# One decoder step on one core: the second feed-forward layer of the last 520 tokens in seven products instead of eight, with low parts of the weights kept from the first half

## The chip, the cores and the metric

One core of a Trainium2 chip runs the whole program. The metric is device time in microseconds (us) of one execution. Three executions of the kernel before took 1424.0, 1428.06 and 1427.56 us; the median is 1427.56 us.

## What is computed

A one-layer decoder on 1024 prompt tokens and 8 sample tokens: an input projection, a gated linear attention and a differential attention beside it (the sample tokens read a paged cache), an output projection, and a feed-forward block. The change touches the last part alone:

```python
    x = x + jnp.einsum('bte,ed->btd', mix, p['w_out'])
    h2 = rmsnorm(x, p['norm_ffn_g'])
    u = jnp.square(jax.nn.relu(jnp.einsum('btd,df->btf', h2, p['w_up'])))
    x = x + jnp.einsum('btf,fd->btd', u, p['w_down'])
```

D_MODEL is 1024, D_FF 4096; all data are fp32.

## The kernel before

**Three products for one.** Each fp32 operand is split into a high part (a copy into fp32r by ScalarE) and a low part (what is left, a subtraction by VectorE). A tile product is then three matmuls, high times high, high times low, low times high (`split_matmuls`, L85 to L87).

**Two blocks of tokens.** Block A is tokens 0 to 511, block B the last 512 prompt tokens and the 8 sample tokens. Inside the program's order comes first the front (input projection, about 430 us), then `feed_forward(part=0)` for A, with attention, recurrence, the keys and the values of the cache done beside it by `beside(tick)` calls, and last `feed_forward(part=1)` for B, with nothing beside it. In B a tile of tokens is two halves p of 256 and 264 columns.

**One block of the feed-forward.** First the output projection, 8 tiles `out`. Then eight groups g: four tiles `up` (x = 0 to 3; 8 k-tiles each, weights `w_up`), and eight tiles `down` (o = 0 to 7; the group's four k-tiles, weights `w_down`), which VectorE adds to the running sum `xt` (L2254). A group of B is 192 matmuls up and 192 down.

**Who makes what, in each group.** SyncE loads the `w_up` tiles into `raw_up` (L1871), ScalarE's queue the `w_down` tiles into `raw_dn` (L2102). For each tile ScalarE makes the high part (`split_high` L2080, `down_high` L2095) and VectorE the low part (`split_low` L2084, `down_low` L2190). After an `up` tile VectorE applies relu and the norm's factor (L2236), ScalarE squares (L2153) and makes the high part `uh` (L2155), VectorE the low part `ul` (L2243). Both blocks split all weights anew.

**What sets the order.** Every engine runs its list in the order in which it is written, and waits on counting semaphores. PSUM has 8 banks; B uses four of them in turn, and a bank is free once VectorE has read it (`take`, `freed`). In B the norm's factors are made behind the first `up` tile: L1975, L2195, L2184 (GpSimd), L2200, L1982, and last the copy `rb2` (L2145), which the first relu waits for.

**Beside A in the last third of its time** run the cached values: 32 units of four 256 KB pages (`vr`, L2555), each unit two groups of four matmuls (L2634); the ring holds two units' pages.

**The end.** `turn_y` transposes `xt` (L2045), ScalarE copies to `y` (L2113; two buffers, so the third copy waits for the first store), SyncE stores (L1896, L1898).

## Time and profile before

| | |
|---|---|
| three executions, us | 1424.0, 1428.06, 1427.56 |
| median, us | 1427.56 |
| profiled execution, span, us | 1424.1 |
| instructions | 23612 |
| TensorE clock granted, mean share | 0.993 |
| moved by DMA | 211.99 MB, mean 149 GB/s |

The profile gives the span of its execution, from the first to the last instruction, and no separate time for it; the span is as long as the shortest of the three executions. PE is TensorE's matmuls, PEld its weight loads, which overlap them, DVE VectorE, ACT ScalarE, POOL GpSimd, SP SyncE; ACTq and SPq are the instructions that issue DMAs. Matmuls are pipelined: each has a duration of about 0.28 us, while the next one starts about 0.12 us later, so the step from start to start is what one costs.

### The profile page before, as it was taken

To read this page: it belongs to the slowest core of one execution; us is meant where nothing else is said; L and a number is where in the kernel's file an instruction comes from. 1 tells how busy PE (TensorE), PEld (TensorE's weight loads), DVE (VectorE), ACT (ScalarE), POOL (GpSimd) and SP (SyncE) were. 2 spreads that over 40 slices of the span, in tenths; PEclk is the share of its full clock that TensorE was granted. 3 is DMA by queue.
4 is the path that set the end of the run, shared out by engine and by line. 5 is a ranking of instruction groups with operands and counts; after the bars stand their busy time and mean duration, and the time that the engine had idled before them with its cause. 6 is when DMAs were issued, how large, how long until landed. Compare 5 with 4: busy or idle time off the path is not lost.

```text
span 1424.1 us, 23612 instructions
## 1 busy us (share of the span) xinstructions
PE 1375.1 (97%) x8781; PEld 1145.8 (80%) x8781; DVE 834.5 (59%) x1416; ACT 542.6 (38%) x1011; POOL 318.1 (22%) x363
## 2 busy tenths in 40 slices
PE   7998999999999999998999999999999999999998
PEld 6767777776777767776767767667999999999998
DVE  5469667745648886758667564444454455445542
ACT  6444332414546554533325241332442234223431
...
GB/s 273 147 129 236 219 131 169 140 120 140 89 159 168 184 174 112 132 165 121 104 240 240 190 218 174 315 245 62 179 125 76 90 119 104 60 75 119 119 31 60
DMA packets 115635, 211.99 MB, mean 149 GB/s; under 512 B 12665, under 2 KB 45722, under 8 KB 115522
## 3 DMA queue, kind: packets, MB, share of 16 engines
...
q14 instruction: 44, 0.36, 0.1%
...
## 4 chain that ended last, share of the span: by engine, by line
PE 64%; DVE 5%; ACT 3%; issue 2%; DMA 0%; ACTq 0%; POOL 0%; SPq 0%; DVEq 0%; POOLq 0%
PE ps L85 18%; PE ps L87 17%; PE ps L86 17%; PE ps L2634 2%; PE ps L1495 2%; PE ps L1532 2%; PE ps L1314 1%; DVE uw_l L2084 1%; PE ps L1516 1%; ACT uw_h L2080 1%; DVE ul L2243 1%; PE ps L1728 1%; DVE sd L2388 1%; DVE dl L2190 1%; DVE xr L2236 0%
## 5 line engine op out<-in xcount | busy, mean ns | idle before, releaser
L85 PE MATMUL ps<-uh,dh 128*128 128x512 f32 (+2 forms) x768 | 250.0, 326 | 5.0 <-DVE dl L2190 3.9
L87 PE MATMUL ps<-uh,dl 128*128 128x512 f32 (+2 forms) x768 | 245.4, 320 | 0.0
L86 PE MATMUL ps<-ul,dh 128*128 128x512 f32 (+2 forms) x768 | 245.0, 319 | 0.0
L2399 POOL TENSOR_TENSOR kr<-kr,qb 128x512 f32<-128x512 f32 x128 | 175.9, 1385 | 167.4 <-DMA kr<-in_cache_k 167.0
L2254 DVE TENSOR_TENSOR xt<-xt,ps 128x256 f32<-128x256 f32 (+2 forms) x192 | 97.6, 512 | 164.6 <-PE ps L87 164.1
L85 PEld LDWEIGHTS ps<-uh,dh 128*128 128x128 f32 x768 | 144.4, 188 | 25.3 <-DVE xt L2254 7.6
L87 PEld LDWEIGHTS ps<-uh,dl 128*128 128x128 f32 x768 | 144.5, 188 | 11.5
L86 PEld LDWEIGHTS ps<-ul,dh 128*128 128x128 f32 x768 | 144.6, 188 | 9.7
L2095 ACT ACTIVATE dh<-raw_dn 128x1024 fp32r<-128x1024 f32 x64 | 67.5, 1055 | 215.6 <-PE ps L87 214.9
L2080 ACT ACTIVATE uw_h<-raw_up 128x1024 fp32r<-128x1024 f32 x80 | 84.5, 1056 | 163.4 <-PE ps L87 163.3
L85 PE MATMUL ps<-x2hB,uw_h 128*128 128x264 f32 (+1 forms) x512 | 145.2, 284 | 0.7 <-DVE x2lB L2218 0.7
L86 PE MATMUL ps<-x2lB,uw_h 128*128 128x264 f32 (+1 forms) x512 | 144.7, 283 | 0.0
L87 PE MATMUL ps<-x2hB,uw_l 128*128 128x264 f32 (+1 forms) x512 | 144.5, 282 | 0.0
L2084 DVE TENSOR_TENSOR uw_l<-raw_up,uw_h 128x1024 fp32r<-128x1024 f32 x80 | 99.7, 1246 | 35.6 <-ACT uw_h L2080 35.5
L85 PE MATMUL ps<-x2hA,uw_h 128*128 128x512 f32 x256 | 106.4, 416 | 0.0
L2388 DVE TENSOR_REDUCE sd<-kr 128x8 f32<-128x512 f32 x128 | 84.9, 675 | 33.2 <-POOL kr L2399 33.1
L87 PE MATMUL ps<-x2hA,uw_l 128*128 128x512 f32 x256 | 101.9, 398 | 0.0
L86 PE MATMUL ps<-x2lA,uw_h 128*128 128x512 f32 x256 | 101.6, 397 | 0.0
L2190 DVE TENSOR_TENSOR dl<-raw_dn,dh 128x1024 fp32r<-128x1024 f32 x64 | 81.0, 1266 | 28.2 <-ACT dh L2095 24.3
L85 PEld LDWEIGHTS ps<-x2hB,uw_h 128*128 128x128 f32 x512 | 96.5, 189 | 0.9 <-DVE x2lB L2218 0.9
L2236 DVE SCALAR_TENSOR_TENSOR xr<-ps,rb 128x256 f32<-128x256 f32 (+1 forms) x96 | 49.0, 514 | 81.1 <-PE ps L87 76.9
L86 PEld LDWEIGHTS ps<-x2lB,uw_h 128*128 128x128 f32 x512 | 96.5, 188 | 0.0
...
## 6 DMA issues: line engine op xcount, KB each, us to landing
kr<-in_cache_k SPq DMA_DIRECT2D x128, 256.0 KB, 3.1
raw_up<-in_w_up_units SPq DMA_DIRECT2D x64, 512.0 KB, 4.7
vr<-in_cache_v SPq DMA_DIRECT2D x128, 256.0 KB, 3.5
raw_dn<-in_w_down ACTq DMA_DIRECT2D x62, 512.0 KB, 3.6
raw<-in_w_in_units SPq DMA_DIRECT2D x23, 512.0 KB, 5.1
raw_up<-in_w_out_units SPq DMA_DIRECT2D x16, 512.0 KB, 4.4
xin<-in_x_prompt SPq DMA_DIRECT2D x8, 512.0 KB, 5.4
xt_scratch<-xts SPq DMA_DIRECT2D x8, 512.0 KB, 5.9
```

The costliest lines, as they stand in the source:

```text
L85: pe.matmul(out, lh, rh, start=first and n == 0, stop=False)
L86: pe.matmul(out, lh, rl, start=False, stop=False)
L87: ins = pe.matmul(out, ll, rh, start=False, stop=last and n == len(ks) - 1)
L1495: pe.matmul(ps[:, score_bank(n, c) + j // 512, 0:x], qt[r, b, i * P:(i + 1) * P], kt[r, b, j:j + x], start=True, stop=j + x < w)
L2080: act.activation(uw_h[:, t % 2, :, :], raw_up[:, t % 2, :].rearrange("p (k c) -> p k c", c=P), ACT.Copy).then_inc(up_high, 1)
L2084: dve.tensor_tensor(uw_l[:, t % 2, :, :], raw_up[:, t % 2, :].rearrange("p (k c) -> p k c", c=P), uw_h[:, t % 2, :, :].bitcast(FP32), ALU. ...
L2095: act.activation(dh[:, x, :], raw_dn[:, x % 2, :], ACT.Copy).then_inc(dn_high, 1)
L2190: dve.tensor_tensor(dl[:, x, :], raw_dn[:, x % 2, :], dh[:, x, :].bitcast(FP32), ALU.subtract).then_inc(dn_low, 1)
L2236: dve.scalar_tensor_tensor(vt[:, i % 2, 0:spans[p][1]], ps[:, bank("up", g, x, p), 0:spans[p][1]], 0.0, rb2[:, tokens(p)], ALU.max, ALU.mu ...
L2254: dve.tensor_tensor(xt[:, o, c], xt[:, o, c], ps[:, bank("down", g, o, p), 0:spans[p][1]], ALU.add).then_inc(added, 1)
L2388: dve.tensor_reduce(m["sd"][:, b, g, :], place(v)[:, :].rearrange("p (h d) -> p h d", d=DH), X, ALU.add).then_inc(k_used, 1)
L2399: pool.tensor_tensor(k[:, :], k[:, :], qb[v // PAGES][:, :], ALU.mult).then_inc(k_multiplied, 1)
```

## The change

**Block B's second layer.** In each group the product of the 4 x 8 tiles of `w_down` and the 4 x 2 tiles of u is done as a 2 x 2 block product with seven block products instead of eight (`PRODUCTS`). A block of weights is 2 k-tiles x 4 output tiles: A11, A12, A21, A22. Three of the seven use A11, A12, A22, four use sums S1 to S4 of blocks. On the other side stand U11, U21, U22 and T1 to T4, differences of blocks of u. A product is four tiles j of 2 k-tiles x 3 matmuls. Some products go onto what is in their bank already (`onto`), after VectorE has added that to `xt`: P6 onto P1, P7 onto P6, P4 onto P7, P3 onto P5. So P6's tile j waits until P1's tile j is added (`product`).

**VectorE** makes the four sums of weights for the next group between the additions (after the additions 4, 10, 16 and 23, counted from 0), and for the first group during `out` 5 and 6. It makes the low parts of the sums, and T1 to T4 with their low parts. The low parts of A11, A12 and A22, and of all `w_up` tiles but the first two, it makes no more: **block A stores them** to HBM (`keep_low`, `load_down`), and block B loads them (`load_low`, `load_kept`). B's `w_down` tiles are loaded by SyncE. In A, `split_low` and `down_low` wait until what they overwrite is stored.

**Around it.** B uses all 8 banks; copies of y have places of their own and are shared between ScalarE and VectorE.

The functions of block A are the old ones with part = 0 written in; what is new in them:

```diff
+        def keep_low(t):
+
+            if t == KT:
+                for i in range(2):
+                    sp.wait_ge(up_out[i], STORED)
+            sp.dma_start(a["up_low"][t - KT], uw_l[:, t % 2, :, :].bitcast(FP32).rearrange("p k c -> p (k c)")).then_inc(up_out[t % 2], 16)
...
-                    load_up(t + 3)
+                load_up(t + 3)
+                if t + 1 < TILES:
+                    keep_low(t + 1)
                 beside(tick)
                 beside(tick + 1)
...
     def split_low(dve, t):
-        dve.wait_ge(up_high, tile_no(t) + 1)
+        dve.wait_ge(up_high, t + 1)
+        if t >= KT + 2:
+            dve.wait_ge(up_out[t % 2], STORED + 16 * ((t - KT) // 2))
         dve.tensor_tensor(uw_l[:, t % 2, :, :], raw_up[:, t % 2, :].rearrange("p (k c) -> p k c", c=P),
                           uw_h[:, t % 2, :, :].bitcast(FP32), ALU.subtract).then_inc(up_low, 1)
 
...
         def load_down(n):
 
...
+            act.wait_ge(dn_low, n - 1)
+            if n == 2:
+                act.wait_ge(dn_out, STORED)
+            last = slice(0, HALF if (n - 2) % FT < 2 else D_MODEL)
+            act.dma_start(a["dn_low"][n - 2, :, last], dl[:, (n - 2) % FT, last].bitcast(FP32)).then_inc(dn_out, 16)
+            f = n % (FT * FGROUPS) * P
+            act.dma_start(raw_dn[:, n % 2, :], a["w_down"][f:f + P, :]).then_inc(dn_in[n % 2], 16)
...
         def down_low(g, x):
-            n = FT * (FGROUPS * part + g) + x
-            dve.wait_ge(dn_high, n + 1)
+            dve.wait_ge(dn_high, FT * g + x + 1)
+            if g and x == 0:
+                dve.wait_ge(dn_out, STORED + 16 * FT * g)
             dve.tensor_tensor(dl[:, x, :], raw_dn[:, x % 2, :], dh[:, x, :].bitcast(FP32), ALU.subtract).then_inc(dn_low, 1)
```

Block B (`feed_last`): the products, the loads, the product on TensorE, and who makes the factors and parts.

```diff
+PRODUCTS = {"P1": ("A11", "U11", "X"), "P2": ("A12", "U21", "Y"), "P3": ("S4", "U22", "Z"), "P4": ("A22", "T4", "X"),
+            "P5": ("S1", "T1", "Z"), "P6": ("S2", "T2", "X"), "P7": ("S3", "T3", "X")}
+BEGINS = ("P1", "P5", "P2")
+AFTER = {"P6": "P1", "P7": "P6", "P4": "P7", "P3": "P5"}
+
+
+def products(g):
+
+    if g == FGROUPS - 1:
+        return [(x, j) for x in ("P1", "P6", "P2", "P7", "P5", "P4", "P3") for j in range(PAIRS)]
+    return ([("P1", j) for j in range(PAIRS)]
+            + [(x, j) for js in ((0, 1), (2, 3)) for x in ("P5", "P6", "P2", "P7", "P3", "P4") for j in js])
...
+    def freed(kind, key):
+        if kind == "out":
+            return x2_made, out_no(*key) + 1
+        if kind == "up":
+            return v_made, up_no(*key) + 1
+        g, x, j = key
+        return added, added_no(g, {"P1": "P4", "P5": "P3", "P2": "P2"}[x], j)
...
+    def sync(sp):
+        def load_up(t):
+            sp.wait_ge(up_low if t - 2 < SPLIT else up_high, tile_no(t) - 1)
...
+        def load_low(t):
+
+            n = t - KT
+            if n == 2:
+                for i in range(2):
+                    sp.wait_ge(lo_in[i], LO0[i])
+                    sp.wait_ge(sem(f"y_out{i}"), 32)
+            else:
+                sp.wait_ge(*tile_done(t - 3))
+            sp.dma_start(low_tile(t).bitcast(FP32).rearrange("p k c -> p (k c)"), a["up_low"][n]).then_inc(lo_in[n % 3], 16)
+
+        def load_kept(g, name):
+
+            k, c = {"A11": (0, 0), "A12": (2, 0), "A22": (2, HALF)}[name]
+            if g:
...
+                sp.wait_ge(down_ready, product_no(g - 1, user, PAIRS - 1))
...
+            sp.dma_start(factor(fl, name).bitcast(FP32), a["dn_low"][FT * g + k:FT * g + k + 2, :, c:c + HALF].rearrange("k p c -> p k c"))\
...
+        def load_down(g, x):
+            f = (FT * g + x) * P
+            sp.dma_start(raw(x), a["w_down"][f:f + P, :]).then_inc(dn_in[x], 16)
...
+        for g in range(FGROUPS):
+            for x in range(FT):
+                t = KT + FT * g + x
+                if KT + 2 < t + 2 < TILES:
+                    load_low(t + 2)
+                if t + 3 < TILES:
+                    load_up(t + 3)
+            if g + 1 < FGROUPS:
+                sp.wait_ge(dn_low, low_sum_no(g, "S4"))
+                sp.wait_ge(dn_high, factor_no(g, "A22"))
+                for x in range(FT):
+                    load_down(g + 1, x)
+                for name in KEPT:
+                    load_kept(g + 1, name)
...
+        def product(g, x, j):
+
+            name, part, kind = PRODUCTS[x]
+            if x in BEGINS:
+                take(pe, "down", (g, x, j))
+            else:
+                pe.wait_ge(added, added_no(g, AFTER[x], j))
+            if j == 0 and name in KEPT:
+                pe.wait_ge(dn_high, factor_no(g, name))
+                pe.wait_ge(kept_in, KEPT0 + 48 * (g + 1))
+            elif j == 0:
+                pe.wait_ge(dn_low, low_sum_no(g, name))
+            f, n = slice(j * P, (j + 1) * P), width(x)
+            for k in range(2):
+                if j == 0:
+                    pe.wait_ge(u_low, low_no(g, part, k))
+                ins = split_matmuls(pe, ps[:, down_bank(g, kind, j), 0:n],
+                                    lambda k: (factor(fh, name)[:, k, f], factor(fl, name)[:, k, f]),
+                                    lambda k: (part_place(part, k, False)[:, 0:n], part_place(part, k, True)[:, 0:n]),
+                                    [k], x in BEGINS and k == 0, k == 1, x not in BEGINS)
+            ins.then_inc(down_ready, 1)
...
+        def high_factor(g, name):
+            if name in ("A11", "A12", "A22"):
+                for x in ((0, 1) if name == "A11" else (2, 3)):
+                    act.wait_ge(dn_in[x], raw_no(g, x))
+            else:
+                act.wait_ge(s_added, sum_no(g, name))
+            if g:
+                user = next(x for x in PRODUCTS if PRODUCTS[x][0] == name)
+                act.wait_ge(down_ready, product_no(g - 1, user, PAIRS - 1))
+            else:
+                act.wait_ge(down_ready, DOWN0)
+                act.wait_ge(kept_in, KEPT0)
+            act.activation(factor(fh, name), factor_source(name), ACT.Copy).then_inc(dn_high, 1)
...
+        for g in range(FGROUPS):
+            t = KT + FT * g
+            more = g + 1 < FGROUPS
+
+            high_factor(g, "A22")
+            if g == 0:
+                split_high(act, t + 2)
+                act.wait_ge(norm_product, 4)
+                for p in range(2):
+                    ins = act.activation(rb2[:, tokens(p)], ps[:, 7 - p, 0:HALVES[p][1]], ACT.Copy)
+                ins.then_inc(rb2_made, 1)
+            high_factor(g, "S1")
+            high_factor(g, "S3")
+            square(g, 0, 0)
+            high_part(g, "U11", 0)
+            square(g, 0, 1)
+            if g:
+                split_high(act, t + 2)
+            high_part(g, "T1", 0)
+
+            high_factor(g, "S2")
+            high_factor(g, "S4")
+            square(g, 1, 0)
+            high_part(g, "U11", 1)
+            square(g, 1, 1)
+            split_high(act, t + 3)
+            high_part(g, "T1", 1)
+
+            square(g, 2, 0)
+            high_part(g, "U21", 0)
+            square(g, 2, 1)
+            if more:
+                split_high(act, t + 4)
+            for name in ("U22", "T2", "T3", "T4"):
+                high_part(g, name, 0)
+
+            square(g, 3, 0)
+            high_part(g, "U21", 1)
```

```diff
+        def summed(g, name):
+
+            a11, a12, a21, a22 = (quarter(x) for x in ("A11", "A12", "A21", "A22"))
+            if name == "S1":
+                for x in range(FT):
+                    dve.wait_ge(dn_in[x], raw_no(g, x))
+                if g == 0:
+                    dve.wait_ge(sem("mix_turned"), 18)
+                    dve.wait_ge(sem("ods_done"), 1)
+                else:
+                    dve.wait_ge(dn_low, low_sum_no(g - 1, "S1"))
+                dst, one, two, op = s1[:, :, :], a21, a22, ALU.add
+            elif name == "S3":
+                dst, one, two, op = a21, a11, a21, ALU.subtract
+            elif name == "S2":
+                dve.wait_ge(dn_high, factor_no(g, "A11"))
+                dst, one, two, op = a11, s1[:, :, :], a11, ALU.subtract
+            else:
+                dve.wait_ge(dn_high, factor_no(g, "A12"))
+                dst, one, two, op = a12, a12, a11, ALU.subtract
+            if name != "S1":
+                dve.wait_ge(s_added, sum_no(g, name) - 1)
+            dve.tensor_tensor(dst, one, two, op).then_inc(s_added, 1)
+
+        def low_factor(g, name):
+            dve.wait_ge(dn_high, factor_no(g, name))
+            if g == 0:
+                dve.wait_ge(out_ready, OUT0 + 2 * KT)
+            dve.tensor_tensor(factor(fl, name), factor_source(name), factor(fh, name).bitcast(FP32), ALU.subtract).then_inc(dn_low, 1)
...
+        def change(g, name, k):
+
+            at_ = lambda x, p: u[:, x, p, :]
+            if name == "T1":
+                dve.wait_ge(u_high, high_no(g, k, 1))
+                dst, one, two = t1[:, k, :], at_(k, 1), at_(k, 0)
+            elif name == "T2":
+                dve.wait_ge(u_high, high_no(g, 2 + k, 1))
+                dst, one, two = t1[:, k, :], at_(2 + k, 1), t1[:, k, :]
+            elif name == "T3":
+                dst, one, two = at_(k, 1), at_(2 + k, 1), at_(k, 1)
+            else:
...
+        def add(g, x, j):
+            dve.wait_ge(down_ready, product_no(g, x, j))
+            o, c = out_tile(x, j)
+            here = [(h, *w) for h in (g - 1, g) if h >= 0 for w in products(h) if out_tile(*w) == (o, c)]
+            if here.index((g, x, j)):
+                dve.wait_ge(added, added_no(*here[here.index((g, x, j)) - 1]))
+            dve.tensor_tensor(xt[:, o, c], xt[:, o, c], ps[:, down_bank(g, PRODUCTS[x][2], j), 0:c.stop - c.start], ALU.add)\
+                .then_inc(added, 1)
...
+            relu(g, 3, 0)
+            relu(g, 3, 1)
+            low_part(g, "U21", 1)
+            change(g, "T2", 1)
+            change(g, "T3", 1)
+            low_part(g, "T2", 1)
+            change(g, "T4", 1)
+            low_part(g, "T3", 1)
+            low_part(g, "U22", 1)
+            low_part(g, "T4", 1)
+            for n, what in enumerate(products(g)):
+                add(g, *what)
+                if g + 1 < FGROUPS and n in (4, 10, 16, 23):
+                    summed(g + 1, SUMS[(4, 10, 16, 23).index(n)])
```

**Where instructions stand.** ScalarE at the start of block B's groups, from the copies of the norm's factors (`rb`) to the high part (`uw_h`) of the fourth `up` tile's weights; before:

```order
L2145 ACTIVATE rb_93<-ps 128x256
L2145 ACTIVATE rb_93<-ps 128x264
L2153 ACTIVATE xr<-xr 128x256
L2155 ACTIVATE uh<-xr 128x256
L2153 ACTIVATE xr<-xr 128x264
L2155 ACTIVATE uh<-xr 128x264
L2102 DMA raw_dn<-in_w_down 128x1024
L2095 ACTIVATE dh<-raw_dn 128x1024
L2080 ACTIVATE uw_h<-raw_up 128x1024
```

and now (`fh` is the high part of a factor, `part_h` that of a part of u):

```order
L2642 ACTIVATE rb_93<-ps 128x264
L2596 ACTIVATE fh<-s_134 128x1024
L2596 ACTIVATE fh<-raw_dn 128x1024
L2601 ACTIVATE u<-u 128x256
L2609 ACTIVATE part_h<-u 128x264
L2601 ACTIVATE u<-u 128x264
L2609 ACTIVATE part_h<-t_138 128x264
L2596 ACTIVATE fh<-raw_dn 128x1024
L2596 ACTIVATE fh<-raw_dn_133 128x1024
L2601 ACTIVATE u<-u 128x256
L2609 ACTIVATE part_h<-u 128x264
L2601 ACTIVATE u<-u 128x264
L2576 ACTIVATE uw_h<-raw_up 128x1024
```

The split (L2080, now L2576) of the fourth `up` tile stood 5 computing instructions behind the copies; now it stands 11 behind them, four of them 1024 elements wide.

VectorE at the turn from a group's `up` tiles to its products, block B; before:

```order
L2236 SCALAR_TENSOR_TENSOR xr<-ps,rb_93 128x264
L2243 TENSOR_TENSOR ul<-xr,uh 128x256
L2243 TENSOR_TENSOR ul<-xr,uh 128x264
L2084 TENSOR_TENSOR uw_l<-raw_up,uw_h 128x1024
L2254 TENSOR_TENSOR xt<-xt,ps 128x256
```

and now (`part_l` is the low part, L2756 makes a T, L2717 a sum of weights, L2769 is the addition that frees a bank for the next product onto it):

```order
L2739 SCALAR_TENSOR_TENSOR u<-ps,rb_93 128x264
L2760 TENSOR_TENSOR part_l_140<-u,part_h 128x256
L2756 TENSOR_TENSOR t_138<-u,t_138 128x264
L2756 TENSOR_TENSOR u<-u 128x264
L2760 TENSOR_TENSOR part_l_140<-t_138,part_h 128x264
L2756 TENSOR_TENSOR u<-u,t_138 128x256
L2760 TENSOR_TENSOR part_l_141<-u,part_h 128x264 x2
L2760 TENSOR_TENSOR part_l_141<-u,part_h 128x256
L2769 TENSOR_TENSOR xt<-xt,ps 128x256 x4
L2769 TENSOR_TENSOR xt<-xt,ps 128x264
L2717 TENSOR_TENSOR s_134<-raw_dn,raw_dn_133 128x1024
L2769 TENSOR_TENSOR xt<-xt,ps 128x264 x3
```

Between the last relu and the first addition stood 3 instructions, now 8; the first sum stands between the fifth and the sixth addition.

## Rows read from the trace of the kernel before

**Rows 1.** The page: busy time of the engines, share of the span, instructions.

```profile
PE 1375.1 (97%) x8781; PEld 1145.8 (80%) x8781; DVE 834.5 (59%) x1416; ACT 542.6 (38%) x1011; POOL 318.1 (22%) x363
```

**Rows 2.** Windows: length, then busy of PE, PEld, DVE, ACT, POOL; clock, DMA share, GB/s.

```profile
430.00:1000.00 570.00, 554.84 (x3093) 414.23 (x3092) 359.70 (x571) 221.00 (x417) 110.09 (x118) 0.99 0.55 179
...
1092.00:1410.00 318.00, 318.00 (x2658) 318.00 (x2657) 154.53 (x274) 100.06 (x168) 0.00 (x0) 1.00 0.25 84
```

**Rows 3.** Timeline of PE in block B, group 1 (start us, us).

```profile
1114.30 0.28 PE L85 MATMUL ps<-uh,dh 128*128 128x256 f32 x1
1137.31 0.28 PE L85 MATMUL ps<-x2hB,uw_h 128*128 128x256 f32 x1
1140.15 0.28 PE L85 MATMUL ps<-x2hB,uw_h 128*128 128x264 f32 x1
1160.32 0.28 PE L85 MATMUL ps<-uh,dh 128*128 128x256 f32 x1
```

**Rows 4.** Timeline of DVE: a narrow one, a wide one, three narrow ones together.

```profile
1179.19 0.42 DVE L2254 TENSOR_TENSOR xt<-xt,ps 128x256 f32<-128x256 f32 x1 [0.98 <-PE ps L87]
...
1196.17 1.22 DVE L2084 TENSOR_TENSOR uw_l<-raw_up,uw_h 128x1024 fp32r<-128x1024 f32 x1 [0.72 <-ACT uw_h L2080]
1072.25 1.08 DVE L2254 TENSOR_TENSOR xt<-xt,ps 128x256 f32<-128x256 f32 x3
```

**Rows 5.** Timeline of ACT at the start of block B's groups.

```profile
1054.23 0.67 ACT L2145 ACTIVATE rb<-ps 128x256 f32<-128x256 f32 x2 [4.79 <-PE ps L1982]
1055.45 0.42 ACT L2153 ACTIVATE xr<-xr 128x256 f32<-128x256 f32 x1 [0.56 <-DVE xr L2236]
...
1058.08 1.04 ACT L2080 ACTIVATE uw_h<-raw_up 128x1024 fp32r<-128x1024 f32 x1
```

**Rows 6.** Timeline of PE: first matmul of the fourth `up` tile, first of `down`, group 0.

```profile
1061.63 0.28 PE L85 MATMUL ps<-x2hB,uw_h 128*128 128x256 f32 x1
1068.17 0.39 PE L85 MATMUL ps<-uh,dh 128*128 128x256 f32 x1 [0.63 <-DVE dl L2190]
```

**Rows 7.** Timeline of the end.

```profile
1415.83 1.97 PE L2045 MATMUL ps<-ident,xt 128*128 128x128 f32 x16 [0.52 <-DVE xt L2254]
...
1420.68 1.01 ACT L2113 ACTIVATE y<-ps 8x1024 f32<-8x1024 f32 x1 [1.78 <-DMA out_y_prompt<-y]
```

**Rows 8.** DMAs in the first 24 us: issue, KB, us to landing; then their issue times.

```profile
st<-in_w_in_units SPq DMA_DIRECT2D x1, 512.0 KB, 7.0
0.80 0.41 SPq L287 DMA_DIRECT2D xin<-in_x_prompt  x1
...
2.69 0.76 SPq L292 DMA_DIRECT2D st<-in_w_in_units  x1
```

**Rows 9.** Windows in block A beside the cached values, and one at the very start.

```profile
890.00:915.00 25.00, 25.00 (x128) 16.73 (x126) 15.19 (x19) 10.26 (x14) 0.00 (x0) 1.00 0.95 333
8.00:10.00 2.00, 0.64 (x3) 0.56 (x4) 1.88 (x3) 2.00 (x3) 0.00 (x0) 1.00 1.03 422
```

**Rows 10.** Block A: two value units on PE, and the loads that SP issues between them.

```profile
897.59 1.07 PE L2634 MATMUL ps<-vr,sd 128*32 128x512 f32 x8
...
904.36 1.07 PE L2634 MATMUL ps<-vr,sd 128*32 128x512 f32 x8
898.39 3.62 SPq L2555 DMA_DIRECT2D vr<-in_cache_v  x4
```

**Rows 11.** DMA from 440 to 1000 us: GB/s in 40 slices; issues, median us to landing.

```profile
GB/s 101 195 169 210 96 277 153 107 68 59 140 222 124 196 178 166 34 112 76 243 226 224 169 263 256 140 244 226 237 200 190 142 276 358 263 193 286 221 1 68
...
vr<-in_cache_v SPq DMA_DIRECT2D x128, 256.0 KB, 3.5
...
raw_dn<-in_w_down ACTq DMA_DIRECT2D x32, 512.0 KB, 3.4
```

**Rows 12.** Block A on ACT: a `raw_dn` load issued, and the high part that needs it.

```profile
896.58 0.33 ACTq L2102 DMA_DIRECT2D raw_dn<-in_w_down  x1
...
903.88 1.04 ACT L2095 ACTIVATE dh<-raw_dn 128x1024 fp32r<-128x1024 f32 x1
```

777 lines of the change are left out of this document (534 added, 243 removed).

## The prediction

> **What bounds the kernel now.** I read the page first: TensorE is busy 97% of the span, VectorE 59% and ScalarE 38% [rows 1]. So a stage's time is its matmuls plus what makes TensorE wait. The windows say where it waits: block A, from 430 to 1000 us, leaves it 15.2 us idle; from 1092 to 1410 us, block B's groups, none, with VectorE at 49% and ScalarE at 31% [rows 2]. There a matmul taken away is time gained, as long as nobody else is late. The timeline gives the price. In group 1 the `down` matmuls run from 1114.30 to 1137.31 us and the `up` ones to 1160.32: 23.01 us each for 192 [rows 3]. Twenty-four matmuls of 256 columns take 2.84 us [rows 3], 0.118 each; the other 96 of 23.01 us are then 0.121 each at 264 columns. The durations of 0.28 us overlap and are not prices.
>
> **TensorE: what goes.** `down` of a group is 96 x 0.118 + 96 x 0.121 = 23.0 us. The seven products are 7 x 4 x 6 = 168 matmuls, P2 and P4 (48) at 256 columns, the others (120) at 264: 48 x 0.118 + 120 x 0.121 = 20.2 us. That is 2.77 us a group, **22.2 us** in eight. Sums of weights and of u cost TensorE nothing.
>
> **VectorE: prices.** A narrow instruction (256 or 264) lasts 0.42 to 0.43 us, a wide one (1024) 1.22; of several ready ones the next starts before the last has ended: three take 1.08 us together, so 0.33 to 0.34 apart [rows 4]; a wide one I take as 1.15. ScalarE: narrow 0.42, wide 1.04 [rows 5]. Per group VectorE then has 4 sums and 4 low parts of sums (wide), 8 relus, 8 T, 14 low parts and 28 additions (narrow): 8 x 1.15 + 58 x 0.36 = 30 us of 43.3. It is not the bound on average; what counts is the turn.
>
> The Trainium skill (VectorE: DVE Perf Modes, section Terms) says that a flush follows every VectorE instruction and the next can't issue until the pipe is empty. The three additions in 1.08 us [rows 4] speak against full durations in a row; by the rule, eight narrow ones at the turn would cost 0.09 us more each, 0.7 us a group and 5 us in all.
>
> **The turn, counted from the end of `up`.** The last relu is VectorE's at 0.04 to 0.47. Square on ScalarE to 0.9, T2 to 1.35, its high part to 1.8, its low part to 2.25; then T4 to 2.6 and the low parts of T3, U22, T4, so that the additions begin at about 3.6 and P1's tile 0 is added at 4.05. TensorE meanwhile does P1 (four tiles, 6 x 0.121 = 0.73 us each) and P5's first two, until 4.2: P6, which goes onto P1, comes just in time. Next, P7 needs P6's tile 0 added. Before it VectorE has four more additions, the sum S1, P5's second and P6's first: 3.6 + 5 x 0.34 + 1.15 + 0.34 + 0.43 = 7.2, and TensorE arrives at 4.2 + 2 x 0.73 + 2 x 0.71 = 7.1. After that additions run ahead of products until the group's end.
>
> S1 needs all four new `w_down` tiles. SyncE issues them behind a raw `up` tile whose buffer ScalarE frees at about -3.8. The trace has such a row of five 512 KB loads at the start: the first issued at 0.80, the last at 2.69 us and landed 7.0 later, 8.9 us in all [rows 8]. So they land at 5.2 with empty queues, and at up to 6.5 behind the low tile that is loaded before them; S1 is due at 5.3. Its lateness is TensorE's wait before P7: 0 to 1.4 us a group. I take 0.6 for the seven groups that make sums, between the ends since a part of the low tile is still under way: **+4.2 us** (0 to 9.8). In the last group P6 follows P1 at once and waits from 2.8 to 4.05: **+1.3** (1 to 2).
>
> **Group 0.** The order rows show the split of the fourth `up` tile behind eleven instructions on ScalarE. The copies of the factors end at 1054.9 [rows 5]. S1's and S3's high parts end at 56.9, their low parts on VectorE at 58.2, the two relus at 58.9; squares, U11 and T1 between the two engines at 60.7; the high parts of S2 and S4 at 62.7, their low parts at 64.0, relus, squares and U11 at 65.7, the split at 1066.8. Before, it was through at 1059.1 [rows 5]. TensorE came to the fourth tile at 1061.63 [rows 6] and will come there at the same time, since six banks hold three tiles: a wait of 5.2 us. It takes the place of the 0.6 us at 1068.17 [rows 6]. **+4.6 us** (3 to 6). In later groups the split is done some 3 us before it is due.
>
> **Block A.** It stores 16 MB of `up` and 12 MB of `down` low parts. No matmul is added. SyncE gets one issue more a tile, behind the load of `raw_up`; POOL's list is the same, the slot of a stored tile is wanted again over 10 us later. Beside the values the DMA engines are at 95% and move 333 GB/s in the 25 us of a group's `up` tiles; the highest I see is 422 GB/s [rows 9]. Four `up` and three `down` stores add some 3.5 MB, 140 GB/s: 473 asked for where 422 go, so loads are late by up to 51 x 25 / 422 = 3.0 us at the end. A unit's pages are issued from 898.39 to 902.0 and land 3.5 later [rows 10, 11]; the unit after the next starts at 904.36 + 6.8 = 911.1, 5.6 us to spare [rows 10]. A `raw_dn` load has 7.3 us from issue to use [rows 12] and takes 3.4 [rows 11]; with a store before it in its queue I estimate 6. So nearly all is covered. If the cover goes, a us late is a us of TensorE. The 15.2 us that TensorE idles now [rows 2] show that the cover isn't perfect elsewhere. **+3 us** (0 to 12).
>
> The highest slice of block A itself is 358 GB/s [rows 11]. If that is its ceiling, the backlog is 115 x 25 / 358 = 8.0 us, 2.4 more than the pages' margin, 10 us over four groups with values (rival 4). The Trainium skill (DMA: Bandwidth & Descriptors, section Specifications) gives about 358 GB/s as the limit of a core's share of HBM, and would make this the forecast; the 422 of rows 9 go past it.
>
> **The end.** With more buffers the copy of the sample rows no longer starts at 1420.68, behind a store [rows 7]. A first transposition (1.0 us) now stands before the three that follow the last addition (1415.83 [rows 7]); the sample rows' are done at about 1419.1, the copy starts there: **-1.4 us** (0 to -2). The output projection of B gets four sums in gaps of VectorE that last 2.4 us a tile: 0.
>
> **The sum.** -22.2 + 4.2 + 1.3 + 4.6 + 3.0 - 1.4 = **-10.5 us**. The profiled execution spans 1424.1 us; it is 3.5 below the median, like the shortest of the three. I take the difference off the median: 1427.56 - 10.5 = 1417.
>
> **The rivals.**
> 1. *The products run freely.* S1's tiles land in time, A hides all its stores: -22.2 + 1.3 + 4.6 - 1.4 = -17.7, 1410 us. For it: the 5.6 us of margin. Against it: S1 is due within 0.1 us of the best landing.
> 2. *VectorE's turn becomes the bound.* If its chain with ScalarE at the turn is 1.5 us longer (instructions without overlap, 0.1 us more at each of some eight hand-overs between engines), P6 waits too, and P7 at its worst: 2.4 us a group more than nothing, 17 in seven, and with +4.6, +1.3, +3 and -1.4 the gain is gone: 1428 minus or plus 3, no difference. For it: TensorE and VectorE meet within 0.1 us twice. Against it: P7's wait also takes in what P6 waited.
> 3. *The stores hold up block A*, the slower side. If the `raw_dn` load behind its store takes over 9.5 us instead of 3.4, it eats its 7.3 us and VectorE's pause of some 2 us before the relu, and each us more stands on TensorE, twice a group. At 10.6 us: 2.2 x 8 = 18 us; 1417 - 3 + 18 = 1432 us. For it: DMA at 95% beside the values. Against it: before 712 us the engines are far from full, 179 GB/s over all of A [rows 2].
> 4. *The ceiling of 358 GB/s beside the values*: -10.5 - 3 + 10 gives 1424 us. For it: no slice of A exceeds it [rows 11]. Against it: the start does [rows 9].
>
> **Chances.** My forecast (1412 to 1421) 0.50; rival 1, 0.17; rival 2, 0.17; rival 3, 0.08; rival 4 and things unseen between 1421 and 1426, 0.08. A measurement of this kernel can tell about 0.3%, 4.3 us, from no change. Faster than 1423.3: the forecast, rival 1 and half of the last, 0.71; same: rival 2 mostly and the rest of the last, 0.20; slower: rival 3 and a little of rival 2, 0.09. The range 1407 to 1426 leaves out rival 3 and half of rival 2.
>
> **What would show it.** (a) In B's groups, the first matmul of a group's products to the next group's first `up`: 20.2 us, plus a wait. (b) The wait stands before P7's first tile, released by an addition, and VectorE before S1 waits for a DMA. (c) One wait of about 5 us at group 0's fourth `up` tile, released by ScalarE's split. (d) Block A from 430 to 1000 us is 3 us longer. (e) `vr` and `raw_dn` land later than 3.5 us. The prediction is wrong if TensorE waits over 2 us in every group of B, or if block A grows by over 12.

## The result and the profile after

The changed kernel takes **1435.89 us** (median of 5 runs, 1431.52 to 1439.04), the kernel before 1425.09 in the runs beside it: ratio 1.0064, 95% interval 1.0046 to 1.0083. It is slower, by some 10 us. The profiled execution spans 1437.3 us, 13.2 more than the one of before.

The page of the changed kernel answers to [rows 1], with the bytes of HBM below it (before: 184.00 MB read, 26.46 written). TensorE is busy 13.5 us less and the span 13.2 longer:

```profile
PE 1361.6 (95%) x8589; PEld 1127.2 (78%) x8589; DVE 907.5 (63%) x1629; ACT 580.6 (40%) x1081; POOL 320.2 (22%) x363
...
HBM read 212.32 MB, written 55.82 MB: 187 GB/s over the span
```

**Where the time lies.** ScalarE's high parts of weight tiles come in the same order in both kernels, so equal ones serve as marks. Timeline of ScalarE before, the last one ahead of block B's norm, then the last group's third tile:

```profile
1048.38 1.06 ACT L2080 ACTIVATE uw_h<-raw_up 128x1024 fp32r<-128x1024 f32 x1 [3.51 <-PE ps L87]
...
1373.40 1.06 ACT L2080 ACTIVATE uw_h<-raw_up 128x1024 fp32r<-128x1024 f32 x1 [4.67 <-PE ps L87]
```

and after:

```profile
1068.77 1.06 ACT L2576 ACTIVATE uw_h<-raw_up 128x1024 fp32r<-128x1024 f32 x1 [3.23 <-PE ps L87]
...
1390.06 1.04 ACT L2576 ACTIVATE uw_h<-raw_up 128x1024 fp32r<-128x1024 f32 x1
```

At the first mark the changed kernel is 20.4 us late, at the second 16.7, at the end 13.2. At the first tile of block A it was 1.6 early. So **block A costs 22.0 us** (forecast 3) and **block B gains 7.2** (forecast 13.5 with the end). Below, "A" is the shift from block A's first tile to the first mark and "B" the shift from there to the end, in one profiled execution each, against the kernel before; neither says anything of what lies ahead of block A, where profiles differ by -2.4 to +3.6 us. Five profiles with the same stores show an A of 14.5 to 22.0, so one profile tells A to some 4 us. Six profiles with the same block B show a B of -7.2 to -8.9. The five executions of the changed kernel itself lie 7.5 us apart, so a smaller difference in time against it rests on the marks.

Windows from block A's first tile to the first mark give block A's account; before, then after (the columns are those of [rows 2]):

```profile
378.39:1048.38 669.99, 651.84 (x3745) 499.29 (x3743) 410.84 (x649) 265.83 (x510) 141.20 (x152) 0.99 0.53 173
376.75:1068.77 692.02, 655.97 (x3745) 500.13 (x3743) 415.63 (x652) 269.81 (x513) 144.08 (x152) 0.99 0.64 214
```

The same 3745 matmul records keep TensorE busy 4.1 us longer, and it stands idle for 36.1 us in place of 18.2: 17.9 and 4.1 make the 22.0.

Windows of the changed kernel in block A, the columns as in [rows 2], the second stretch beside the cached values:

```profile
430.00:712.00 282.00, 266.56 (x1411) 206.21 (x1411) 203.46 (x270) 128.94 (x267) 105.42 (x108) 0.99 0.58 190
712.00:1000.00 288.00, 271.38 (x1552) 190.84 (x1551) 148.99 (x288) 88.44 (x140) 6.13 (x8) 0.98 0.77 266
```

The same windows before:

```profile
430.00:712.00 282.00, 271.12 (x1428) 210.30 (x1427) 206.43 (x273) 130.39 (x272) 103.13 (x108) 0.98 0.46 145
712.00:1000.00 288.00, 283.72 (x1667) 203.93 (x1666) 153.27 (x298) 90.61 (x146) 6.96 (x10) 1.00 0.64 212
```

TensorE's idle time was 10.9 and 4.3 us and is 15.4 and 16.6; the second stretch also reaches less far into the work, 1552 matmul records for 1667. The first three rows of its waits between 430 and 1000 us (us in total, times, the longest; `vr` are the pages of the values):

```profile
PE ps L3219 <- DMA vr<-in_cache_v: 13.8, 9, 2.4
PE ps L85 <- DVE dl L2111: 4.7, 4, 1.6
PE ps L85 <- DVE xt L2161: 3.6, 4, 2.1
```

Before, value units waited 0.7 us for their pages in all of the block. Three of the nine waits, then the busy times in windows of 5 us around them:

```profile
909.25 1.06 PE L3219 MATMUL ps<-vr,sd 128*32 128x512 f32 x8 [0.96 <-DMA vr<-in_cache_v]
917.89 1.07 PE L3219 MATMUL ps<-vr,sd 128*32 128x512 f32 x8 [1.79 <-DMA vr<-in_cache_v]
933.62 1.51 PE L3219 MATMUL ps<-vr,sd 128*32 128x512 f32 x8 [2.13 <-DMA vr<-in_cache_v]
```

```profile
908.00:913.00 5.00, 4.04 (x22) 2.42 (x21) 1.99 (x3) 1.06 (x1) 0.00 (x0) 1.00 1.06 410
913.00:918.00 5.00, 3.21 (x18) 2.27 (x20) 3.55 (x4) 3.27 (x4) 0.00 (x0) 1.00 1.03 403
...
928.00:933.00 5.00, 3.49 (x20) 2.18 (x12) 0.93 (x2) 0.69 (x1) 0.00 (x0) 1.00 1.03 404
933.00:938.00 5.00, 4.38 (x23) 2.58 (x24) 0.29 (x1) 0.00 (x0) 0.00 (x0) 0.66 0.81 262
```

For 25 us the DMA engines are full, at 403 to 419 GB/s. Landings from 440 us on grow for nearly every kind (the first two had 3.5 and 3.4 us in [rows 11]):

```profile
vr<-in_cache_v SPq DMA_DIRECT2D x128, 256.0 KB, 4.3
...
raw_dn<-in_w_down ACTq DMA_DIRECT2D x32, 512.0 KB, 7.1
```

The wait at 933.62 can be followed to its pages. SyncE issues a unit's four pages in two pairs, a pair in each step, and the unit starts when all four are there. The second pair of the unit at 933.62 is the first half of this row, issued at 924.30; a wait for room in the ring lies inside the row, ahead of the next unit's pair:

```profile
924.30 6.42 SPq L3140 DMA_DIRECT2D vr<-in_cache_v  x4
```

The view of `vr` from 924.2 to 926.2 us, who waited for this pair (us, times) and how long it took to land:

```profile
PE ps L3219: 2.1, 1
...
DMA to landing us min/median/max: 7.5/7.7/7.8
```

The kernel before was already close to this. There the pages issued first at 898.39 [rows 10] belong to the unit that starts at 904.36, not to the one after the next. The same view from 898.3 to 900.3 us, and the unit's start:

```profile
PEld ps L2634: 0.4, 1
...
DMA to landing us min/median/max: 4.6/4.6/4.7
```

```profile
904.36 0.16 PEld L2634 LDWEIGHTS ps<-vr,sd 128*32 128x32 f32 x8 [0.37 <-DMA vr<-in_cache_v]
```

The second of the pair, issued at 899.48, landed 4.7 us later, at 904.2. Four of the 32 units started within 0.6 us of the landing of their last page.

In block B, TensorE waits at the places that were named. Timeline of TensorE at group 0's fourth `up` tile, and before P7 in group 1; then VectorE's sum S1 in front of that:

```profile
1087.09 0.58 PE L85 MATMUL ps<-x2hB,uw_h 128*128 128x256 f32 x1 [4.92 <-ACT uw_h L2576]
...
1148.18 0.39 PE L85 MATMUL ps<-part_h,fh 128*128 128x264 f32 x1 [1.54 <-DVE xt L2769]
```

```profile
1146.23 1.22 DVE L2717 TENSOR_TENSOR s<-raw_dn,raw_dn 128x1024 f32<-128x1024 f32 x1 [1.52 <-DMA raw_dn<-in_w_down]
```

The long wait costs more than itself. The window behind it has TensorE at half its clock (0.50, its level of 1.2 GHz):

```profile
1087.00:1091.00 4.00, 3.91 (x18) 3.91 (x19) 2.57 (x7) 3.13 (x9) 0.00 (x0) 0.50 0.71 243
```

### The profile page after: what moved, and what is told of

Read it like the earlier page. It is cut to its first block, busy times and chain, and to the rows that moved or that the text cites. A ratio compares the mean times of both kernels' runs of the same rounds, so it can differ in the third digit from the quotient of the medians.

```text
span 1437.3 us, 23957 instructions
## 1 busy us (share of the span) xinstructions
PE 1361.6 (95%) x8589; PEld 1127.2 (78%) x8589; DVE 907.5 (63%) x1629; ACT 580.6 (40%) x1081; POOL 320.2 (22%) x363
## 4 chain that ended last, share of the span: by engine, by line
PE 49%; DMA 8%; DVE 7%; issue 4%; ACT 4%; SPq 3%; POOL 1%; ACTq 0%; DVEq 0%; POOLq 0%
PE ps L85 14%; PE ps L87 13%; PE ps L86 13%; DMA raw_dn<-in_w_down 3%; DMA vr<-in_cache_v 3%; PE ps L3219 2%; DVE uw_l L2019 1%; PE ps L1495 1%; SPq L3139 1%; PE ps L1314 1%; PE ps L1532 1%; ACT uw_h L2013 1%; DMA kr<-in_cache_k 1%; DVE sd L2973 1%; SPq L2438 1%
## 5 line engine op out<-in xcount | busy, mean ns | idle before, releaser
L85 PE MATMUL ps<-part_h,fh 128*128 128x264 f32 (+1 forms) x448 | 127.8, 285 | 7.8 <-DVE xt L2769 7.8
L87 PE MATMUL ps<-part_h,fl 128*128 128x264 f32 (+1 forms) x448 | 127.0, 284 | 0.0
L86 PE MATMUL ps<-part_l,fh 128*128 128x264 f32 (+1 forms) x448 | 126.8, 283 | 0.0
L85 PE MATMUL ps<-uh,dh 128*128 128x512 f32 x256 | 106.2, 415 | 8.3 <-DVE dl L2111 4.7
L2769 DVE TENSOR_TENSOR xt<-xt,ps 128x264 f32<-128x264 f32 (+1 forms) x224 | 86.7, 422 | 24.7 <-PE ps L87 23.9
L87 PE MATMUL ps<-uh,dl 128*128 128x512 f32 x256 | 101.6, 397 | 0.0
L86 PE MATMUL ps<-ul,dh 128*128 128x512 f32 x256 | 101.3, 396 | 0.0
L87 PEld LDWEIGHTS ps<-x2hB,uw_l 128*128 128x128 f32 x512 | 97.2, 190 | 0.0
L85 PEld LDWEIGHTS ps<-part_h,fh 128*128 128x128 f32 x448 | 84.5, 189 | 9.4 <-DVE xt L2769 9.2
L86 PEld LDWEIGHTS ps<-part_l,fh 128*128 128x128 f32 x448 | 84.3, 188 | 0.0
```

The source lines that it names most:

```text
L85: pe.matmul(out, lh, rh, start=first and n == 0, stop=False, skip_group_check=onto)
L86: pe.matmul(out, lh, rl, start=False, stop=False, skip_group_check=onto)
L87: ins = pe.matmul(out, ll, rh, start=False, stop=last and n == len(ks) - 1, skip_group_check=onto)
L2769: dve.tensor_tensor(xt[:, o, c], xt[:, o, c], ps[:, down_bank(g, PRODUCTS[x][2], j), 0:c.stop - c.start], ALU.add)\
```

## The experiments

All 18, with A and B as above and the time against the kernel before as it ran beside them (medians of the kernel before: 1425.8 in the first four, 1427.5 in the next four, 1426.3 to 1426.4 then):

| run | MB written | A | B | time | to before | 95% of the ratio |
|---|---|---|---|---|---|---|
| the changed kernel | 55.8 | +22.0 | -7.2 | 1435.89 | +10.8 | 1.0046 to 1.0083 |
| no_stores | 28.6 | +3.2 | -8.1 | 1417.67 | -8.1 | 0.9925 to 0.9958 |
| a_stores_only | 55.8 | +14.5 | -0.1 | 1440.44 | +14.7 | 1.0092 to 1.0128 |
| no_up_stores | 39.6 | +7.6 | -8.9 | 1424.28 | -1.5 | 0.9975 to 1.0 |
| half_stores | 42.2 | +7.7 | -7.7 | 1426.59 | +0.8 | 0.9998 to 1.0028 |
| group0_order | 55.8 | +16.3 | -9.3 | 1433.08 | +5.5 | 1.0024 to 1.0064 |
| gpsimd_lows | 28.0 | -0.2 | +49.1 | 1476.68 | +49.1 | 1.0309 to 1.0374 |
| gpsimd_group0 | 28.0 | -0.7 | +46.2 | 1470.78 | +43.2 | 1.0273 to 1.0333 |
| s1_later | 28.6 | -0.4 | -15.8 | 1413.06 | -14.5 | 0.9884 to 0.9938 |
| early_stores | 41.1 | +4.0 | -7.8 | 1423.22 | -3.1 | 0.996 to 0.9986 |
| late_stores | 41.1 | +9.1 | -8.1 | 1429.81 | +3.4 | 1.0015 to 1.0039 |
| late_sums_group0 | 55.8 | +17.7 | -20.4 | 1422.97 | -3.4 | 0.9968 to 1.0004 |
| gpsimd_two_tiles | 47.4 | +11.0 | -11.3 | 1424.15 | -2.2 | 0.9977 to 1.0 |
| gpsimd_tiles_a11 | 43.8 | +10.8 | -4.4 | 1434.49 | +8.1 | 1.0039 to 1.0074 |
| dve_two_tiles | 46.9 | +7.1 | 0.0 | 1429.52 | +3.1 | 1.0002 to 1.0031 |
| dve_tiles_a22 | 43.2 | +3.2 | +3.1 | 1430.57 | +4.2 | 1.0006 to 1.0033 |
| dve_four_a22 | 35.4 | +2.3 | +9.3 | 1441.27 | +14.9 | 1.008 to 1.0116 |
| down_first | 55.8 | +18.5 | -13.4 | 1430.41 | +4.1 | 1.0016 to 1.0035 |
| dve_a22_down_first | 43.2 | +3.2 | -16.8 | **1412.49** | **-13.8** | 0.9891 to 0.9921 |

Six of these are no whole kernels: no_stores, no_up_stores, half_stores, early_stores, late_stores and s1_later leave low parts unstored, and block B reads others in their place. They show times only.

### Is it the stores, and their bytes?

**no_stores.** Only the first tile's and the first group's low parts are stored.

```diff
-                if t + 1 < TILES:
-                    keep_low(t + 1)
...
-            act.dma_start(a["dn_low"][n - 2, :, last], dl[:, (n - 2) % FT, last].bitcast(FP32)).then_inc(dn_out, 16)
+            if n - 2 < FT:
+                act.dma_start(a["dn_low"][n - 2, :, last], dl[:, (n - 2) % FT, last].bitcast(FP32)).then_inc(dn_out, 16)
...
-            sp.dma_start(low_tile(t).bitcast(FP32).rearrange("p k c -> p (k c)"), a["up_low"][n]).then_inc(lo_in[n % 3], 16)
+            sp.dma_start(low_tile(t).bitcast(FP32).rearrange("p k c -> p (k c)"), a["up_low"][0]).then_inc(lo_in[n % 3], 16)
```

> Leaves out all stores of low parts behind the first tile and the first four row blocks, and block B reads the first group's low parts in every group, so its loads keep their number and size. Theory A (the stores' traffic costs block A its time): block A's end goes back from +22 us to within 4 us of the kernel before, DMA writes fall by about 26 MB, and with block B's own gain of 7 us the time is 1417 to 1421 us. Theory B (the loss in block A has another source, such as the split of one function into two or where the queues stand): at least 10 us of the 22 stay, 1428 us or more. Theory C (block B's loads of the stored parts cost block B something): nothing moves in B by this run, since its loads stay; it shows in neither.

18.9 us less than the changed kernel, each against the kernel before as it ran beside it (the last columns; so are all differences below). Block A's loss is the stores'; its new waits and split function cost at most the 3 us that are left, which s1_later, with the same block A, doesn't show.

**a_stores_only.** Block B is the old function again:

```diff
-        fB = feed_last(nc, a, m, ps, sem, at)
+        fB = feed_old(nc, a, m, ps, sem, at, 1)
```

> Block A as in the changed kernel, stores and their waits included; block B as in the kernel before, so nothing reads what is stored. If the two blocks' parts add up, block A's +22 us stands alone here: 1445 to 1449 us, and block B's landmarks all lie 20 to 22 us behind the kernel before. If part of the 22 us came from work that block B's new code pulled forward into block A, it is under 1440 us.

The loss stands alone: B's marks stay at +13.4 us to the end. The number missed: A is 14.5 here, less than the 20 to 22 expected; that is where A's scatter was first seen. The times bear the adding up less well than the marks, 3.9 us between this run and the changed kernel where B gives 7.2.

**no_up_stores.** As no_stores, but all `dn_low` stores stay.

> Leaves out the stores of the up weights' low parts but for one tile (30 of 30.5 stores of 512 KB on SP's queue); those of w_down's low parts stay (12 MB on ACT's queue). Block B reads the first tile's low part for every tile. If volume is what costs, each kind has its share by its bytes: 16 of the 28 MB gone leaves 40 to 50% of block A's loss, 9 to 11 us, so 1425 to 1428 us. If the stores' place ahead of the cached values' pages on SP's queue is what costs, nearly all of the loss goes: 1417 to 1420 us. If it is the stores ahead of the w_down loads on ACT's queue, nearly nothing goes: 1433 us or more.

1424.28, just under the volume theory's price, 12.3 us less than the changed kernel. Neither theory of a queue's order gives that.

**half_stores.** Every store and wait stays; from the second group on (the second `up` tile on) a store is half as wide; for `w_down`:

```diff
-            last = slice(0, HALF if (n - 2) % FT < 2 else D_MODEL)
+            last = slice(0, (HALF if (n - 2) % FT < 2 else D_MODEL) // (2 if n - 2 >= FT else 1))
```

> Every store stays, at its place and with its waits, but from the second group on writes only the first half of its columns; block B reads the first group's low parts in every group. Volume theory: half of block A's loss goes, or more, since the engines then have room beside the cached values: 10 to 16 us less than the changed kernel, 1420 to 1426 us. Order theory (a transfer ahead of the pages in its queue delays them whatever its size, or the new waits hold up the queues): at most 3 us less, 1432 us or more.

10.0 us less with the same number of stores and waits, at the lower edge of the volume theory and far from the 3 us of the other. It is the bytes.

**early_stores** (its edit for `up`) and **late_stores** store one half of the groups, whole:

```diff
-                if t + 1 < TILES:
+                if t + 1 < KT + 16:
                     keep_low(t + 1)
```

> The low parts of groups 0 to 3 are stored in block A, whole, as in the changed kernel; those of groups 4 to 7 are not, and block B reads the first four groups' twice. So it writes the same half as half_stores, but none of it beside the cached values. If the cost is the traffic beside the values (where the engines were full), block A loses 2 to 4 us and block B goes as in no_stores: 1417 to 1421 us. If a stored byte costs the same wherever it falls, block A loses the 6.7 us of half_stores or more (its stores are denser): 1425 us or more.

> The other half of early_stores: only the low parts of groups 4 to 7 are stored, whole, most of them beside the cached values; block B reads these twice. If the traffic beside the values is what costs, block A loses 12 to 18 us, three to four times the 3.8 us of early_stores for the same bytes, and the time is 1430 to 1435 us. If bytes cost the same everywhere (or the early ones only set up what is lost later), 4 to 8 us and 1421 to 1426 us.

Over no_stores, 12.6 MB cost 5.0 us before the values and 11.5 mostly beside them, each to some 3 us; the two add up to 16.5 of the 18.9 of all stores. The waits of value units for pages follow: 1.6 us in two waits, 9.5 in seven (5.7 in four with half_stores, 13.8 in nine with all). So a byte costs about twice as much in the stretch where the engines are fuller (64% busy before, 46% in the other), but it isn't free elsewhere. Both runs lie between their theories: early_stores 1423.22 with 1417 to 1421 and 1425 or more named, late_stores with 9.1 in block A under the 12 to 18 expected.

### Block B's own steps

**group0_order** moves two high factors in the first group ahead of the wait:

```diff
                 split_high(act, t + 2)
+                high_factor(g, "S1")
+                high_factor(g, "S3")
                 act.wait_ge(norm_product, 4)
```

> The changed kernel, with ScalarE's high parts of S1 and S3 in block B's first group moved ahead of its wait for the norm's product, where it idles 4.8 us (in the changed kernel they run behind that wait, VectorE makes their low parts before the first two relus, and these start 3.4 us late). Theory D (this order costs block B's first group most of its +7.5 us): the landmark of the first group's fourth up tile comes 2.5 to 5 us sooner, block B as a whole gains 3 to 6 us on the changed kernel, about 1430 us from its 1435.9 (block A's own scatter of some 3 us lies on top). Theory E (the first group is late for its stored low parts or its weights, not for this order): under 1 us.

The wait for the fourth tile falls from 4.92 to 1.72 us; block B gains 2.1 of the 3 to 6 expected, hardly more than the scatter of B (the time, 5.3 less, has A's scatter in it), since P7's wait in this group grows from 0.89 to 2.24. **s1_later** takes that on, on top of no_stores:

```diff
-                if g + 1 < FGROUPS and n in (4, 10, 16, 23):
-                    summed(g + 1, SUMS[(4, 10, 16, 23).index(n)])
+                if g + 1 < FGROUPS and n in (7, 11, 16, 23):
+                    summed(g + 1, SUMS[(7, 11, 16, 23).index(n)])
```

> As no_stores, with VectorE's sum S1 behind the eighth of a group's additions in place of the fifth, and S3 behind the twelfth in place of the eleventh. Theory G (in groups 1 to 4 the sum waits up to 2.0 us for its w_down tiles, and the additions behind it then hold up TensorE): the step of these groups gains 1 to 2 us each, 3 to 6 us in all, 1412 to 1415 us. Theory H (the wait is only handed on to S3 and S2, or VectorE's turn is too full for a later sum): within 1.5 us of no_stores, either way.

Theory G and more: B is 7.7 us better, and each step from group 1 to group 7 is 2.71 us shorter than before, where it was 1.50 in the changed kernel. **late_sums_group0** is both edits with all stores:

> The changed kernel, whole, with two orders of block B changed: S1 behind the eighth and S3 behind the twelfth addition (7.6 us in s1_later), and the first group's high factors ahead of the norm (2.2 us in group0_order). If the two add up with the stores in place, 9 to 10 us less than the changed kernel: 1425 to 1428 us, level with the kernel before. If the later sums only paid where no stored parts were late, under 5 us less, 1431 us or more.

14.2 us under the changed kernel, where 9 to 10 was expected, and no product waits any more in a later group but in the last (1.13 us). Timeline of TensorE, group 1's first product, its end and the next `up`:

```profile
1130.85 0.28 PE L85 MATMUL ps<-part_h,fh 128*128 128x264 f32 x1
...
1151.14 0.28 PE L85 MATMUL ps<-x2hB,uw_h 128*128 128x256 f32 x1
```

20.29 us for seven products: the forecast of 20.2.

**down_first** changes no sum; it issues the `w_down` loads earlier in SyncE's list.

```diff
                 if t + 3 < TILES:
                     load_up(t + 3)
+                if x == 1 and g + 1 < FGROUPS:
...
+                    for y in range(FT):
+                        load_down(g + 1, y)
```

> The changed kernel with that one move alone: the w_down loads 5 to 8 us sooner, sums and first group as they were. If S1 behind the fifth addition was late only for its w_down tiles, block B's steps go to 2.7 us a group (from 2.0 on the mean) and the time is 5 to 7 us under the changed kernel, 1428 to 1431 us. If the early sum itself delays the additions that the sixth product waits for, under 2 us.

Steps 2.52 us shorter than before in place of 1.50; B gains 6.2 us, the time 6.7. SyncE's queue in the changed kernel, then here (this group's marks are 3.9 us earlier here):

```profile
1180.61 0.33 SPq L2403 DMA_DIRECT2D raw_up<-in_w_up_units  x1
1181.04 2.71 SPq L2438 DMA_DIRECT2D raw_dn<-in_w_down  x4
```

```profile
1168.89 1.76 SPq L2438 DMA_DIRECT2D raw_dn<-in_w_down  x4
...
1171.39 0.33 SPq L2403 DMA_DIRECT2D raw_up<-in_w_up_units  x1
```

The buffers were free at least 8 us before; the loads stood behind an `up` load that waited for its own.

### Fewer bytes: who makes the low parts instead?

**gpsimd_lows** and, with the order of group 0, **gpsimd_group0**; GpSimd makes the low parts of A11, A12 and A22 too, with an instruction that isn't shown:

```diff
+            pool.tensor_tensor(low_tile(t), raw_up[:, t % 2, :].rearrange("p (k c) -> p k c", c=P),
+                               uw_h[:, t % 2, :, :].bitcast(FP32), ALU.subtract).then_inc(low_tile_in(t)[0], 16)
```

> No low parts are stored or read back but those of w_down's first four row blocks; GpSimd, idle in block B, makes the other ones there: 30 up tiles and three quarters a group, 128x1024 each. An estimate of 2.8 us for one, twice the 1.39 us of its 128x512 operations, gives 19 us a group of 44. Theory A (traffic was all that block A lost): block A within 4 us of the kernel before, DMA bytes back to about 212 MB less what block B no longer does, 1415 to 1418 us. Theory F (traffic's cost only turns into another: GpSimd and VectorE slow each other, VectorE's instructions get over 15% longer and its turn between the additions and the next factors sets the pace): block B takes 2 us a group more, 1425 us or more.

> Both of the two edits above. If D and A hold and they add up: 1410 to 1414 us, 11 to 15 us under the kernel before. If GpSimd's work and the earlier factors get in each other's way in the first group, it is within 1 us of the one without the order.

Block A is whole again, and block B loses 49 and 46 us: theory F, and more. GpSimd takes 2.40 us for a tile, but holds VectorE up. Timelines of GpSimd and of VectorE in gpsimd_lows:

```profile
1221.50 2.40 POOL L2683 TENSOR_TENSOR uw_l<-raw_up,uw_h 128x1024 fp32r<-128x1024 f32 x1 [4.85 <-PE ps L87]
```

```profile
1221.71 2.47 DVE L2775 TENSOR_TENSOR part_l<-t,part_h 128x264 fp32r<-128x264 f32 x1 [0.80 <-ACT part_h L2591]
```

An instruction of 0.43 us lasts 2.47, to 0.3 us behind the end of GpSimd's. Between 1150 and 1350 us the mean of this kind is 1.44 us for 16. The order of group 0 gains 2.9 us in B here, so the two edits get in each other's way no more than in the changed kernel. **gpsimd_two_tiles** and **gpsimd_tiles_a11** leave GpSimd less of it, mostly beside additions, on top of late_sums_group0:

> late_sums_group0, and GpSimd makes the low parts of the first two up tiles of each group behind the first, during the products, where VectorE mostly reads PSUM; only the other two are stored. Block A writes 8 MB less. Theory I (GpSimd holds up VectorE only where VectorE's instruction has both operands in SBUF): block B within 3 us of late_sums_group0, block A 3 to 6 us better, 1420 to 1424 us. Theory J (it holds VectorE up for its own 2.4 us each time): 14 x 2 us are lost in block B, over 1435 us.

> gpsimd_two_tiles, and GpSimd makes the low part of A11 too (21 of 24 kept quarters become 14; 4 MB less are written in block A, 4 MB less read in B). Theory I: another 1 to 3 us less than gpsimd_two_tiles, 1418 to 1422 us, which would beat both kernels. Theory J or a late A11 in front of the sum S2: slower than gpsimd_two_tiles by 3 us or more.

The steps are 1.49 and 0.55 us shorter than before in place of 2.71, and B is 9.1 and 16.0 us worse than in late_sums_group0. The bytes saved in A are paid back in B: theory I, which allowed 3 us, falls, though J's 28 us are not lost either.

**dve_two_tiles** lets VectorE make two tiles a group in gaps between relus, **dve_tiles_a22** also A22's low part, **dve_four_a22** all four tiles:

```diff
             relu(g, 2, 0)
+            low_tile_made(KT + FT * g + 3)
             relu(g, 2, 1)
```

> late_sums_group0, and VectorE makes the low parts of two of a group's four up tiles in block B itself (the fourth, and the next group's first), in the 2.4 and 1.5 us in which it waits for TensorE between two relus; only the other two are stored and read back, 8 MB less each way. If these gaps are free, block B keeps its step of 2.7 us a group and block A loses 8 to 13 us in place of 17.5: 1414 to 1419 us. If VectorE's turn is full (each 1.2 us lands on TensorE), block B gives back 8 times 2.4 us and it is 1430 us or more.

> dve_two_tiles, and VectorE makes A22's low part as well, in its wait of 1.7 us for the high part of S1 at a group's start; 4 MB less are stored and 4 MB less read. If that gap is free too, block A wins another 1 to 3 us and block B loses under 1: 1412 to 1417 us, the best so far. If the 0.5 us that stick out move S1's low part and the first relus, the group's step grows by 0.5 us, and it is level with dve_two_tiles.

> No low part of an up tile is stored; VectorE makes all four a group in block B and A22's: three in the gaps between relus (0.9, 2.4 and 1.5 us) and one ahead of the additions. Only A11 and A12 are stored, 8 MB in all. Block A loses 3 to 6 us. Block B: the tile ahead of the additions has no gap and costs 1.2 us a group, the one in 0.9 us another 0.3, so some 12 us of its 20 are given back: 1417 to 1423 us. If the turn takes it up in its waits during the products, 1408 to 1412 us.

All three missed in block B. For the first two the gaps are free: the first addition of every group comes 3.56 us behind the start of the last relu, as in late_sums_group0. But S1 now waits 3.24 us for its tiles, since an `up` load in front of them in SyncE's list now waits for VectorE's low part:

```profile
1226.42 1.23 DVE L2728 TENSOR_TENSOR s<-raw_dn,raw_dn 128x1024 f32<-128x1024 f32 x1 [3.24 <-DMA raw_dn<-in_w_down]
```

**dve_a22_down_first** puts the `w_down` loads ahead, as in down_first, and nothing else:

> dve_tiles_a22, with the next group's four w_down loads in SP's list behind the second up tile's loads in place of the fourth's. In dve_tiles_a22 the sum S1 waits 3 to 4 us a group for them: they stand behind a load_up that waits for VectorE's low part of the tile before. Theory K (VectorE's gaps are free and only this place in the queue cost the 2 us a group): the step of a group goes back to 2.7 us under the kernel before, block B gains 12 to 14 us on dve_tiles_a22, block A keeps its 3 us: 1410 to 1414 us, 12 to 16 under the kernel before. Theory L (VectorE's turn itself is full, its waits for w_down only show where it ends): S1 no longer waits but the step stays within 0.7 us of dve_tiles_a22, 1425 us or more.

Theory K. The step is 2.71 us shorter again, B -16.8, A +3.2, and the time 18.0 us under dve_tiles_a22: **1412.49 us, 13.8 under the kernel before and so 24.6 better than the change**, with the whole computation done. What dve_four_a22 would give with the same move stays open. The page of dve_a22_down_first:

```profile
PE 1356.0 (96%) x8589; PEld 1126.8 (80%) x8589; DVE 929.1 (66%) x1651; ACT 580.3 (41%) x1081; POOL 320.2 (23%) x363
```

## Why the prediction was wrong

The forecast was 1417.0, the range 1407 to 1426; the result, 1435.89, lies above it. Against the 1425 that the kernel before has in later runs, forecast -10.5, measured +10.8.

**Block A, +3: the step that failed is the cover.** Measured 14.5 to 22.0 in five profiles. The demand was read rightly: 473 GB/s asked, and the engines did move 403 to 419. The size of a delay was right too: 3.0 us, and the longest wait for pages is 2.4. What failed is "5.6 us to spare". It gives the pages issued from 898.39 on to the unit that starts at 911.1, and takes the 3.5 us of the median for their landing. The first two of them are the last pages of the unit at 904.36, took up to 4.7 us, and were there 0.2 us before that unit. So the spare time was 0.2 us in the place that was looked at, and nine units stood open to a lateness that was counted once, for the 25 us of one group. And only the fullest 25 us were counted; the early half of the stores, where the engines were at 46%, still cost 5.0 us.

The other margin held. `raw_dn` took up to 9.6 us, but the load that did had 11.3 us from issue to use; those with about 7.4 us took 5.0 to 7.5, and one of them met its use (0.02 us to spare). Rival 3's price, `raw_dn` behind its store, did come up (7.1 for 3.4 us in the median, 10.6 supposed) but isn't the main part. TensorE stands idle 17.9 us longer; between 430 and 1000 us 13.1 of them are waits for the pages and 3.4 those for `dl` and `xt`. The other 4.1 us are its longer busy time, part of which is its clock, below. How the pages' and the other waits came to differ from profile to profile isn't settled.

**Rival 4** had the mechanism, pages late beside full engines, at 10 us, but by a ceiling that isn't there (358 GB/s, where windows show 403 to 419) and with the same margin of 5.6 us; its result of 1424 is too low too. The Trainium skill (Perfetto Trace Analysis, section Engine Utilization) allows a single active core about 435 GB/s from its 16 DMA engines; 403 to 419 in full windows agrees.

**TensorE, -22.2.** Right: 2.71 a group where nothing waits (forecast 2.77), eight times 21.7.

**The turn, +4.2.** P7 waits behind S1 for the `w_down` tiles, as said; the six steps from group 1 on lost 1.21 us each (2.71 - 1.50), where 0.6 was taken from 0 to 1.4. P6 came just in time in every group but the last. SyncE's five loads were issued 3.7 us before the end of `up` in group 1, for 3.8 forecast, but the last landed 8.9 to 10.9 us after the first was issued, where 8.9 was taken; and the list could have issued them 8 us sooner, as down_first shows. The VectorE walk itself held: 3.56 us from the last relu to the first addition, 3.6 forecast. The rule of a flush after each instruction would have added 0.7 us; nothing here shows it.

**Group 0, +4.6.** The wait is there with 4.92 us (5.2 forecast). But by TensorE's own starts the group lost 7.4 us in all: the first `up` of group 0 is 20.2 us late (1061.63 for 1041.46), that of group 1 24.9 (1116.19 for 1091.29), and 2.7 were saved in between. Not in the sum: half the clock in the 4 us behind the wait, 2.0 us; 0.9 before P7; 0.2 in the first tile. With the 0.63 saved [rows 6], 7.4.

**The last group and the end** (+1.3, -1.4 with -2.77): -2.7 for -2.87, right. P6's wait in it is 1.13 us.

So block B gave 7.2 us of 13.5, and block A took 22 where 3 were allowed. The chance of 0.09 for slower was too low: the forecast and rivals 1, 2 and 4 all stood on the same margin of 5.6 us. That block B's sum came out 6.3 us too good has its own two causes, the turn and group 0; it did not offset anything.
